# One weight load for both halves of a float32r activation: two matmuls over 256 columns become one over 512

## What is computed

```python
# first block
h = modulate(rms_norm(x, norm1_g), shift1, scale1)      # shift, scale, gate: silu(c) @ w_ada + b_ada
lru_x, lru_gate, q, k, v, g_a, g_b = split(h @ w_in)    # 2048 -> 10752
y_a = (rg_lru(conv(lru_x)) * gelu(lru_gate)) @ w_lru_out
y_b = windowed_attention(q, k, v, sinks, rel_bias) @ w_attn_out
x = x + gate1 * ((sigmoid(g_a) * y_a + sigmoid(g_b) * y_b) @ w_out)
h2 = modulate(rms_norm(x, norm2_g), shift2, scale2)
x = rms_norm(x + gate2 * (square(relu(h2 @ w_ff1)) @ w_ff2), final_g)   # 2048 -> 8192 -> 2048
# second block, two layers
for l in range(2):
    parts = split(x @ w_in[l])          # queries, keys, values, gates of three kinds of attention
    y = concat(fox(...), dsa(...), memory(...)) * silu(gates)
    x = layer_norm(ALPHA * x + y @ w_out[l])
```

## Time and profile before

| | us |
|---|---|
| median of 3 runs | 2824.92 |
| lowest, highest | 2823.28, 2825.01 |
| the profiled execution | 2825.39 |
| its span | 2823.5 |
| TensorE busy in it | 2725.1 (97%) |
| VectorE busy | 1858.0 (66%) |
| ScalarE busy | 1340.4 (47%) |
| mean granted TensorE clock | 0.986 of full speed |
| weights read | 574 MB, 204 GB/s |

### The profile page before, as it was taken

One profiled execution on the slowest core, in us unless ns is written; L12 is line 12 of the kernel. 1 busy time (PEld: TensorE's weight loads), 2 busy tenths in 40 slices (PEclk: granted clock), 3 DMA queues, 4 the chain that ended last, 5 costly groups with the idle time before them and its releaser, 6 DMA issues.

```text
span 2823.5 us, 52496 instructions
## 1 busy us (share of the span) xinstructions
PE 2725.1 (97%) x22266; PEld 2676.5 (95%) x22266; DVE 1858.0 (66%) x2581; ACT 1340.4 (47%) x1942; POOL 142.2 (5%) x177
## 2 busy tenths in 40 slices
PE   4789999999999999999999999999999999999997
PEld 4789899999999999999999999999999999999997
DVE  7987977876788865555555556566465665664655
ACT  3355555554444554444444444444554454445543
POOL 0000000000001000000000010100000131000002
PEclk8899999999999999999999999999999999999998
DMA  8955677778889875555555555555445555554453
GB/s 334 373 207 165 206 240 252 246 258 271 285 297 326 271 236 180 181 187 185 182 184 183 184 183 164 183 179 177 153 150 181 193 174 180 179 173 157 149 170 107
DMA packets 162154, 584.86 MB, mean 207 GB/s; under 512 B 19041, under 2 KB 20321, under 8 KB 161793
## 3 DMA queue, kind: packets, MB, share of 16 engines
q1 hardware_dynamic: 157104, 566.86, 60.6%
q0 software_dynamic: 4528, 12.43, 1.4%
q10 hardware_dynamic: 288, 2.23, 0.2%
HBM read 574.05 MB, written 2.15 MB: 204 GB/s over the span
## 4 chain that ended last, share of the span: by engine, by line
PE 90%; DVE 9%; ACT 1%; issue 0%; DMA 0%; SPq 0%; ACTq 0%; DVEq 0%
PE bank L663 26%; PE bank L664 25%; PE bank L665 25%; DVE raw L1336 3%; PE bank L671 2%; PE bank L672 2%; PE bank L673 2%; DVE wlo L1295 2%; PE pS L706 1%; PE pO L729 1%; PE pT L718 1%; DVE XC L1749 1%; PE pS L759 1%; DMA CR<-in_c 0%; DVE MM L1443 0%
## 5 line engine op out<-in xcount | busy, mean ns | idle before, releaser
L1295 DVE TENSOR_TENSOR wlo<-raw,whi 128x1024 fp32r<-128x1024 f32 (+1 forms) x880 | 1080.1, 1235 | 709.3 <-ACT whi L920 707.0
L920 ACT ACTIVATE whi<-raw 128x1024 fp32r<-128x1024 f32 (+1 forms) x880 | 923.0, 1052 | 766.9 <-PE bank L665 690.5
L663 PE MATMUL bank<-Hhi,whi 128*128 128x256 f32 x4096 | 1176.8, 287 | 54.4 <-DVE Hlo L1376 49.0
L664 PE MATMUL bank<-Hlo,whi 128*128 128x256 f32 x4096 | 1163.9, 284 | 0.0
L665 PE MATMUL bank<-Hhi,wlo 128*128 128x256 f32 x4096 | 1163.4, 284 | 0.0
L663 PEld LDWEIGHTS bank<-Hhi,whi 128*128 128x128 f32 x4096 | 790.9, 193 | 66.7 <-issue 57.6
L664 PEld LDWEIGHTS bank<-Hlo,whi 128*128 128x128 f32 x4096 | 791.3, 193 | 0.6
L665 PEld LDWEIGHTS bank<-Hhi,wlo 128*128 128x128 f32 x4096 | 790.8, 193 | 0.0
L663 PE MATMUL bank<-Fh,whi 128*128 128x256 f32 x1024 | 289.8, 283 | 0.0
L664 PE MATMUL bank<-Fl,whi 128*128 128x256 f32 x1024 | 289.8, 283 | 0.0
L665 PE MATMUL bank<-Fh,wlo 128*128 128x256 f32 x1024 | 289.8, 283 | 0.0
(11 more groups left out here) (314 smaller groups left out, 3419.8 us busy)
## 6 DMA issues: line engine op xcount, KB each, us to landing
raw<-in_w_in SPq DMA_DIRECT2D x424, 512.0 KB, 3.7
raw<-in_w_ff SPq DMA_DIRECT2D x256, 512.0 KB, 3.7
raw<-in_ada SPq DMA_DIRECT2D x192, 512.0 KB, 5.2
raw<-in_w_out SPq DMA_DIRECT2D x96, 512.0 KB, 4.4
raw<-in_w_lru_out SPq DMA_DIRECT2D x32, 512.0 KB, 4.5
raw<-in_w_attn_out SPq DMA_DIRECT2D x32, 512.0 KB, 5.1
raw<-in_w_kv SPq DMA_DIRECT2D x32, 512.0 KB, 4.4
BT<-gtab POOLq DMA_DIRECT2D x32, 128.0 KB, 4.0
```

The lines of the kernel that those rows point to most:

```text
L663: pe.matmul(o, h, xh[:, kt, :], start=start, stop=False, skip_group_check=True)
L664: pe.matmul(o, h, xl[:, kt, :], start=False, stop=False, skip_group_check=True)
L920: act.activation(whi[:, s, 0:el.n], raw[el.slot][:, 0:el.n], ACT.Copy).then_inc(s_hi, 1)
L1295: dve.tensor_tensor(wlo[:, s, 0:n], raw[el.slot][:, 0:n], v32(whi[:, s, 0:n]), ALU.subtract).then_inc(s_lo, 1)
```

## The change

For each slice k and block i, `whi` was loaded twice, once for the high half of the activation and once for the low half. Now the two halves of every activation lie in one tensor (`H`, `Z`, `G`, `M0`, `M1`, `F2`, `YY`), and one matmul of 512 columns reads both through an access pattern with two pieces of 256. Its result fills a whole bank: 256 columns of high x high and 256 of high x low. The third product adds into the half of the high part. So a unit of mode "f" takes two banks, one for each block, and the banks are two pairs. At its end ACT copies one half of both banks to a spare SBUF tile (`EB`, `EP` or `ET`, places that are free then), and DVE adds the other half to it and writes the first bank, where the evacuation reads the unit's result as before. pM is given up for the fourth bank; its users go to pT. Modes "t" and "s" and `lrux` are as they were.

```diff
@@ _plan
-            un.bank = turn % 3
+            un.bank = 2 * (turn % 2)
             turn += 1
-        un.after = holder.get(un.bank, ())
+            if un.mode == "f":
+                un.wide = n_wide
+                n_wide += 1
+        un.after = holder.get(un.bank // 2, ())
@@ _build
-    Hhi, Hlo = at("Hhi", [128, NB, S], o_h, F32R), at("Hlo", [128, NB, S], o_h + 16384, F32R)
+    H = at("H", [128, 2, NB, S], o_h, F32R)
+    Hhi, Hlo = H[:, 0, :, :], H[:, 1, :, :]
...
+    EB, EP, ET = (at(n, [128, 2, S], off) for n, off in (("EB", o_bt + 2048), ("EP", o_pt), ("ET", o_tg + 3 * 2048)))
...
-    bank = [nc.alloc_psum_tensor(f"bank{i}", [128, 512], F32) for i in range(3)]
+    bank = nc.alloc_psum_tensor("bank", [128, 4, 512], F32)
     pS2 = nc.alloc_psum_tensor("pS2", [128, 2, 512], F32)
     pS = pS2[:, 0, :]
-    pT, pO, pM = (nc.alloc_psum_tensor(f"p{i}", [128, 512], F32) for i in "TOM")
+    pT, pO = (nc.alloc_psum_tensor(f"p{i}", [128, 512], F32) for i in "TO")
...
+    def half_banks(un, half):
+
+        return bank[:, un.bank:un.bank + 2, 256 * half:256 * half + 256]
+
+    def spare(un):
+
+        if un.kind in ("q", "k"):
+            return EB
+        return EP if un.kind in ("km", "ff1") or un.kind == "res" and un.n >= 8 else ET
@@ tensor
+        def products_wide(un, c):
+
+            ch = un.chunks[c]
+            s = ch % NSP
+            pe.wait_ge(s_lo, split_no[order[ch]])
+            xh, _, both = tensors[un.x]
+            low_first = un.x in ("Y0", "Y1")
+            for i in range(2):
+                o = banks[un.bank + i]
+                high = o[:, 256:512] if low_first else o[:, 0:256]
+                for k in range(4):
+                    kt = 4 * un.corder[c] + k
+                    if begins[un.x] is un and i == 0:
+                        pe.wait_ge(*ready[un.x](kt))
+                    at_ = k * 256 + i * 128
+                    pe.matmul(o.rearrange("p (a s) -> p a s", a=2), whi[:, s, at_:at_ + 128], both[:, :, kt, :],
+                              start=(c == 0 and k == 0), stop=False, skip_group_check=True)
+                    ins = pe.matmul(high, wlo[:, s, at_:at_ + 128], xh[:, kt, :], start=False,
+                                    stop=(c == un.nkc - 1 and k == 3), skip_group_check=True)
+            ins.then_inc(s_mm, 1)
...
-                        clear("M")
+                        clear("T")
...
-                            h, o = 2 * job.b + i, pM[:, i * 256:i * 256 + 256]
+                            h, o = 2 * job.b + i, pT[:, i * 256:i * 256 + 256]
@@ scalar, evac
-            if kind not in ("ya", "yb", "res", "y"):
+            if un.wide < 0:
                 act.wait_ge(s_mm, un.chunks[-1] + 1)
+            else:
+                act.wait_ge(s_mm, un.chunks[-1] + 1)
+                if un.wide:
+                    act.wait_ge(s_sum, un.wide)
...
+                act.activation(spare(un)[:, :, :], half_banks(un, 0 if kind == "y" else 1), ACT.Copy).then_inc(s_e, 1)
+                if kind not in ("ya", "yb", "res", "y"):
+                    act.wait_ge(s_sum, un.wide + 1)
@@ vector, evac
+            if un.wide >= 0:
+
+                dve.wait_ge(s_e, un.wide + 1)
+                dve.tensor_tensor(ps.rearrange("p (b s) -> p b s", b=2), half_banks(un, 1 if kind == "y" else 0),
+                                  spare(un)[:, :, :], ALU.add).then_inc(s_sum, 1)
+                if kind in ("ya", "yb", "res", "y"):
+                    dve.wait_ge(s_sum, un.wide + 1)
@@ gpsimd, attention
             pool.wait_ge(s_lg, 16)
+            pool.wait_ge(s_ev["k"], 1)
             load_bias(0)
```

More of the change, by code:

```diff
@@ L64 @@
     after: tuple = ()
+    wide: int = -1
     chunks: list = field(default_factory=list)
@@ L452, in _build @@
     CQ, SMALL = at("CQ", [128, 2, 6], o_acc + 2816), at("SMALL", [128, 6, 16], o_acc + 2880)
-    bank = [nc.alloc_psum_tensor(f"bank{i}", [128, 512], F32) for i in range(3)]
+    bank = nc.alloc_psum_tensor("bank", [128, 4, 512], F32)
     pS2 = nc.alloc_psum_tensor("pS2", [128, 2, 512], F32)
     pS = pS2[:, 0, :]
-    pT, pO, pM = (nc.alloc_psum_tensor(f"p{i}", [128, 512], F32) for i in "TOM")
-    banks = [bank[0], bank[1], bank[2], pS, pS2[:, 1, :], pO, pT, pM]
+    pT, pO = (nc.alloc_psum_tensor(f"p{i}", [128, 512], F32) for i in "TO")
+    banks = [bank[:, i, :] for i in range(4)] + [pS, pS2[:, 1, :], pO, pT]
     gdram = nc.dram_tensor("gtab", (32, 384), F32, kind="Internal").ap()
@@ L484, in _build @@
     s_ev = {k: sem(f"ev_{k}") for k in kinds}
+    s_e, s_sum = sem("e"), sem("sum")
     s_vc = sem("vc")
@@ L863, in tensor @@
                 if st[1] == "bias":
[L864 removed]
+                    clear("T")
                     pe.wait_ge(s_hot, 32)
[L866 to L867 removed]
+                    pe.matmul(pT[0:32, 0:384], relb[:, :], hot[:, :], start=True, stop=True).then_inc(s_gt, 1)
+                    held["T"] = (s_gsb, 1)
                 elif st[1] == "gates":
@@ L883, in tensor @@
                 pe.wait_ge(s_ev[un.after[0]], un.after[1])
-            elif un.part == "open" and un.bank == 3:
+            elif un.part == "open" and un.bank == 4:
                 clear("S")
             for c in range(un.nkc):
-                products(un, c)
+                if un.wide < 0:
+                    products(un, c)
+                else:
+                    products_wide(un, c)
                 if c < un.nkc - 1:
@@ L891, in tensor @@
                 continue
-            if un.part and un.bank > 2:
-                held["SSOTM"[un.bank - 3]] = (s_ev["lrux"], un.n + 1)
+            if un.part and un.bank > 3:
+                held["SSOT"[un.bank - 4]] = (s_ev["lrux"], un.n + 1)
             if un.kind == "res" and (un.n < 8 or un.n >= 64) and un.n % 8 == 7:
@@ L1111, in small @@
             act.wait_ge(s_tkp, l + 1)
-            act.activation(TK[:, :, :], pM[:, 0:172].rearrange("p (t c) -> p t c", t=2)[:, :, 64:86], ACT.Copy).then_inc(s_tk, 1)
+            act.activation(TK[:, :, :], pT[:, 0:172].rearrange("p (t c) -> p t c", t=2)[:, :, 64:86], ACT.Copy).then_inc(s_tk, 1)
             yield
@@ L1803, in evac @@
                 l, j = j // 8, j % 8
-                dve.wait_ge(s_mm, un.chunks[-1] + 1)
                 if l and j == 0:
```

80 lines of the change are left out of this document (41 added, 39 removed).

## The result

| | us |
|---|---|
| before, median of 20 runs (lowest, highest) | 2824.47 (2823.17, 2825.35) |
| after, median of 20 runs (lowest, highest) | 2828.84 (2823.25, 2843.32) |
| ratio after / before, 95% interval | 1.0028 [1.0014, 1.0041] |
| profiled execution of after, its span | 2823.62, 2821.7 |

The change makes the kernel slower by 0.3%. The forecast was 2762 with a range from 2708 to 2812, so it was wrong in size and in sign. The runs of after also don't lie around one value: eleven are between 2823.3 and 2829.1 (median 2824.7), nine between 2836.7 and 2843.3 (median 2839.6), and none between; before spreads over 2.2 us. So 0.3% is the median over a mixture: the lower group is level with before (2824.7 against 2824.5), the upper one 15 us slower. The profiled execution is one of the lower eleven, so its time stands for that group.

What follows compares the result with a forecast made beforehand. PE was taken to set the pace nearly everywhere, with DVE close behind until about 1000 us. 2825.4 less 82.3 saved plus 18.4 of losses gave 2761.5, forecast 2762 us, range 2708 to 2812.

Steps and rivals of the forecast that it cites:

- 346.7 ns, 13.3 less, and 6176 x 13.3 = 82.3 us saved: PE, wide units: a pair takes 226.7 plus 120.0 ns, overhead paid once per matmul; 82.3 us saved.
- Rival 3: Wide matmuls: only part of the 13.3 ns is per matmul, slot 232.4 ns; 47 us saved, 2796 us; chance 0.09.
- Rivals 1 (216 ns) and 4 (240 ns): Wide matmuls: stream hides its load, 2710 us, chance 0.19; or priced by columns, nothing saved, 2844 us, chance 0.09.
- The first 187 us (`lrux`) have no wide unit: Opening `lrux` stage: no wide unit there, and no loss was counted for it.
- Two pairs for three banks ...: 0, since each has a unit of 5 us or more as its cover: Bank pairs and waits at first units: 0 lost; without cover, at most one delay of 1.4 us each.
- Rival 2: Before 1000 us: DVE becomes the bound, sums waiting in order for copies; 23 us saving gone, 2783 us; chance 0.13.
- DVE between 400 and 1000 us: Stretch 400 to 1000 us: DVE 92% busy, in-order waits take 5 us of the 23 that PE saves.
- The scan: Scan, 303 to 337 us: three uncovered sums (2.1 us) and PE's lost saving on three units (1.3); +3.4 us.
- The norm ahead of ff1: Norm, 929 to 962 us: sums and lost saving 3.4, more matmuls behind the last slice 1.0, a copy 0.7; +5.1 us.
- The norm between the layers: Norm, 2250 to 2260 us: one sum and one copy's delay; +1.5 us.
- The end: From the last matmul to the last instruction: nothing runs beside the copy and sum; +1.4 us.
- pT for pM: Six places of the two layers: pM's users share pT, a matmul waits for the transposes' copy; +2 us.

Runs made afterwards that it cites:

- e8: After without the `lrux` pieces' bank-pair wait, q sums written straight to `AT`, and eight wide matmuls before eight narrow ones per chunk: 2788.14 us.
- e4: After without the copies on ACT and sums on DVE, so part of the computation is left out: 2799.97 us.
- e9: After without the `lrux` bank-pair wait, q sums written to `AT`, four wide then four narrow matmuls, `y` halves added directly to the residual: 2795.02 us.
- e3: Before with only the users of bank pM moved to pT: 2825.51 us.
- e2: After with each wide matmul issued as two of 256 columns, each with its own load: 2876.71 us.
- e5: After without the `lrux` bank-pair wait, each block's four wide matmuls issued before its four narrow ones: 2806.52 us.
- e10: e8 with the `y` units' copy and sum dropped, DVE adding both bank halves directly to the residual: 2786.99 us.
- e11: e10 with the 72 residual units also losing copy and sum, DVE adding each bank half directly: 2785.74 us.
- e7: After without the `lrux` bank-pair wait, wide and narrow still alternating, but k outside and the block inside: 2812.61 us.

## Why the prediction was wrong, step by step

Three terms failed: the saving of the wide matmul (82.3 us forecast, 52 to 55 measured), `lrux` (0 forecast, 24 measured), and copies and sums (16.4 forecast, 32 measured). One by one:

- **"346.7 ns, 13.3 less, and 6176 x 13.3 = 82.3 us saved": right for the feed-forward part of some executions only.** There the slots were 230.0 and 116.6 where 226.7 and 120.0 had been written, with the sum as forecast. Elsewhere a pair mostly took 353.3, and 52 to 55 us were saved, or 37 to 41 in the upper group. Rival 3 had 7.6 ns a pair and 47 us saved; its size was nearly right, its reason (a share of the overhead that belongs to the load) was not, since a row of wide ones with the same loads comes down to 226 or 227 in e8, not 232.4. What went wrong was to add up slots of one kind, all measured in a stream without alternation. Rivals 1 (216 ns) and 4 (240 ns) are out. The Trainium skill, "TensorE: Matmul & The Clock Gate", section "Back-to-back issue gap", gives N/2.4 + 2.5 ns for an isolated gap, 215.8 for 512 columns, and about 131 ns for one in a sustained stream; this case's traces disagree with both, at 230 to 237 in alternation and 226 at the least in a row.
- **"The first 187 us (`lrux`) have no wide unit": true, and the wrong question.** The diff changes `un.after` for every unit. I had followed the new divisor for the wide units, not for the pieces that hold one bank each. 24 us; the four waits stand in the order list of after (the one below and three like it; before, no `lrux` matmul waits for `s_ev_lrux`), where they could have been seen.

```order
617 L690 MATMUL bank<-H,whi 128x256 [waits s_lo,s_ev_lrux]
```

- **"Two pairs for three banks ...: 0, since each has a unit of 5 us or more as its cover": wrong for q.** The same holds for "that is the same 1.4 us". The sum isn't done 1.4 us after the last matmul but when DVE comes to it, in order: 4 us after it, at 233.9 us. Rival 2 was this mechanism in part (a sum stands behind what DVE has in hand), but placed between 400 and 1000 us. There PE was busy for 100% up to 900 us with DVE at 78 to 89%, and nothing was lost.
- **DVE between 400 and 1000 us, "5 us of the 23": none up to the last `yb`.** From the first `siga` to the last `yb` after takes 480.3 us and e4, without sums, 480.9. The 83 us of DVE per 100 that the term starts from is the stretch at 800 us; over the 600 us before had 79 and after 85.
- **The scan, "+3.4": somewhat low.** From the first scan to the first `siga` before takes 37.2 us, after 40.8 and e4 37.1. The sums thus cost 3.7 where 2.1 were forecast; the other 1.3 of the term, PE's saving that is lost there, is borne out by e4, which is no shorter than before.
- **The norm ahead of ff1, "+5.1": about right, but with a price behind it.** From where the chain leaves PE to the last slice, before takes 34.0 us (928.0 to 962.0), after 37.4 (951.2 to 988.6), +3.4; of the 5.1 forecast 1.3 were PE's saving of three units, which is lost beside it. The prediction named a lower clock after 960 us as a sign that a stall left at 1 us had grown, and it came: PE waits 2.0 us for the last slice, before 1.3, and the granted clock is 0.50 from 990.1 to 993.5, where before has 1.00. That is 1.7 us of the 4.4 lost in the feed-forward part.
- **The norm between the layers, "+1.5": 0.6 to 0.9.** From the last `y` of the first layer to the last slice of the norm before takes 51.1 us, after 51.7, e4 50.9. The layers lost 9.0 to copies and sums, in the waits of PE told above, for which the prediction had nothing but the 2 us for pT.
- **The end, "+1.4": +3.0.** From the last matmul to the end before takes 21.3 us, after 24.3. Copy and sum are 1.3 of it. The rest is PE. The chain at the end, of after and then of before:

```profile
2794.78 0.13 PE bank L728
...
2798.43 1.44 PE pS L851 x4
2799.87 3.12 PE pT L862 x8
...
2818.82 0.40 ACTq L2074
```

```profile
2801.96 1.13 PE pS L803 x4
2803.09 1.74 PE pT L814 x8
```

  The granted clock from 2799.9 to 2803.0 is 0.58, behind 3.5 us of the chain without a matmul, where before stays at 1.00 behind 2.1 us. The length of the stall alone doesn't decide it: in e8 the chain is without a matmul for 3.5 us too, from 2760.88, and the clock stays at 1.00; in e9 it is 2.9 us, and the same eight records take 3.12 us as in after. The chain of e8:

```profile
2764.40 1.13 PE pS L858 x4
2765.53 1.74 PE pT L869 x8
```

  So 1.7 of the 3.0 us are a price of the clock that the prediction didn't have, and what decides when it falls due isn't shown.
- **pT for pM, "+2": 1.2 alone (e3)**, which can't be told from nothing; but beside the sums the waits on pT came to 3.8 us.
- **"The wide matmul saves, the additions hide": the page could not refute it.** PE is busy for the whole of the stretch in both the 346.7 slot (300.00 of 300 us) and the 353.3 slot (100.00 of 100). The Trainium skill, "Perfetto Trace Analysis", section "Identifying the Most-Contended Engine", says that matmul busy share is a poor measure of the distance to the peak and weight-load busy share a better one. The trace agrees with the first half: the number of instructions in a stretch tells the slots apart, the busy share doesn't. The second half shows little here, 86.7% at 800 us against 88.2% at 1000 us.
- "What would show it" had the slot between 222 and 230 ns as the condition; 230.0 to 236.7 refuted it. PE's waits on `wlo` were some 11 us in all, so the other condition was met.

## What to carry to other kernels

When the number of banks per unit changes, follow each line that maps a bank to its holder for every kind of unit, also for those that the change leaves alone. A slot measured in a uniform stream doesn't hold for a mixture: count instructions per 100 us in each stage of the mixed stream, and group equal matmuls. A result that passes through two engines that work in order comes when the slower queue gets to it, not after the sum of two durations; let the engine that adds write the final place.

## What was not expected of the hardware

- **An alternation of a 512-column and a 256-column float32r matmul, each with its own 128x128 load, takes 346.7 or 353.3 ns at full clock.** It keeps the one or the other through hundreds of microseconds, and by the groups of runs, executions of the same program differ in it. In all samples the value changed only where PE had stalled or run other matmuls in between. What chooses it was not found. Two of 256 columns in place of the wide one are 120.0 each (e2).
- Grouped by four wide and four narrow ones, the same work takes 350.8 in every stretch of the traces of e5 and e9 where nothing else runs, by eight 349.2 in those of e8, e10 and e11. The grouped kernels spread over 0.6 to 2.0 us, the alternating ones over 16 to 20, e7 aside.
- A wait of 4 to 5 us in `lrux` is followed by matmuls 0.21 us apart: the granted clock is 0.61 from 159.0 to 165.4 us and 0.53 from 172.4 to 178.0. The four waits are 19.7 us and cost 24: the matmuls behind each run at half clock.
- Two stalls of one length can differ in that. At the end of the program the granted clock falls behind 3.5 us without a matmul in after and behind 2.9 in e9, and stays at 1.00 behind 3.5 in e8.
